# Attention in units of two heads on different rows of TensorE, and compression in four column groups

## The reference, cut to what matters

```python
# per layer; 4 MLA heads (96 for q and k), 4 differential heads of 2 maps (32), 8 NSA heads in 2 groups (64)
mla:   p = softmax(causal(q_h . k_h));                o_h = p @ v_h
diff:  p_m = softmax(causal(q_hm . k_hm)), m = 0, 1;  o_h = (p_0 - lam * p_1) @ v_h;  o_h = rms_norm(o_h) * (1 - lam_init)
nsa:   k_cmp, v_cmp = compress(k), compress(v)        # 31 blocks of 32 tokens, step 16
       o_cmp = softmax(q_h . k_cmp_g) @ v_cmp_g
       o_slc = softmax(causal(q_h . k_slc_g)) @ v_slc_g   # all 8 blocks of 64 tokens are selected at 512 tokens
       o_win = softmax(causal(q_h . k_win_g)) @ v_win_g
       o_h   = gate_0 * o_cmp + gate_1 * o_slc + gate_2 * o_win
compress: silu(blocks(31, 32*64) @ w1(2048, 256) + b1) @ w2(256, 64)    # for 2 groups, keys and values
out = concat(mla, diff, nsa) @ w_out
```

## Time and profile before

| | |
|---|---|
| median of 3 runs | 4109.87 us (4105.91 to 4119.1) |
| the profiled execution | 4141.39 us, span 4139.6 us |
| TensorE busy | 3912.5 us, 95% |
| VectorE, ScalarE, GpSimdE busy | 1468.9, 1291.3, 1271.3 us |
| mean granted TensorE clock | 0.93 |
| attention of layer 0, from its first score to its last value product | 603.3 to 925.9 us |
| attention of layer 1 | 1910.1 to 2222.8 us |

### The profile page before, as it was taken

How to read it: one execution, slowest core, us unless ns; L and a number is a source line. 1 busy time by engine, 2 the same in 40 slices (tenths; PEclk the granted TensorE clock), 3 DMA queues, 4 the chain that set the end, 5 groups by cost and what they waited for, 6 DMA issues and landing times. The chain is left out here.

```text
span 4139.6 us, 51715 instructions
## 1 busy us (share of the span) xinstructions
PE 3912.5 (95%) x18310; PEld 3064.2 (74%) x18310; DVE 1468.9 (35%) x2542; ACT 1291.3 (31%) x1995; POOL 1271.3 (31%) x524
## 2 busy tenths in 40 slices
PE   7998999999999999899999999699999898878998
PEld 6887666668887888656667888588888686557886
DVE  4224445444224322444445332611111602453112
ACT  4223233324223322313333322421212324334222
POOL 4444220004444444321001444222222242003443
PEclk9999996779999999997679999899999899989999
DMA  4333232102333333323111333222221232002331
GB/s 131 97 97 90 77 103 82 52 26 87 96 97 97 92 96 92 91 78 102 62 62 46 97 96 91 67 64 63 61 61 56 61 87 76 26 21 79 97 97 62
DMA packets 568999, 322.45 MB, mean 78 GB/s; under 512 B 30234, under 2 KB 563328, under 8 KB 568448
## 3 DMA queue, kind: packets, MB, share of 16 engines
q1 hardware_dynamic: 568832, 320.29, 26.5%
HBM read 318.14 MB, written 2.10 MB: 77 GB/s over the span
## 5 line engine op out<-in xcount | busy, mean ns | idle before, releaser
L796 POOL TENSOR_TENSOR w_lo<-w_raw,w_hi 128x1024 fp32r<-128x1024 f32 x516 | 1267.5, 2457 | 2833.3 <-ACT w_hi L807 2833.3
L807 ACT ACTIVATE w_hi<-w_raw 128x1024 fp32r<-128x1024 f32 x516 | 546.8, 1060 | 1901.2 <-PE psum L2001 1817.5
L2001 PE MATMUL psum<-h_hi,w_hi 128*128 128x512 f32 x1328 | 542.9, 409 | 46.2 <-DVE h_ctx_lo L1362 22.1
L2001 PE MATMUL psum<-xg_hi,w_hi 128*128 128x512 f32 x1408 | 551.7, 392 | 11.9 <-DVE xg_lo L1315 10.2
L2001 PE MATMUL psum<-xg_lo,w_hi 128*128 128x512 f32 x1408 | 548.9, 390 | 0.0
L2001 PE MATMUL psum<-xg_hi,w_lo 128*128 128x512 f32 x1408 | 548.8, 390 | 0.0
L2001 PE MATMUL psum<-h_lo,w_hi 128*128 128x512 f32 x1328 | 528.6, 398 | 0.0
L2001 PE MATMUL psum<-h_hi,w_lo 128*128 128x512 f32 x1328 | 526.6, 397 | 0.0
L2001 PE MATMUL psum<-a_hi,w_hi 128*128 128x512 f32 x1232 | 433.3, 375 | 4.9 <-DVE a_lo L1430 4.2
L2001 PE MATMUL psum<-a_lo,w_hi 128*128 128x512 f32 x1232 | 434.1, 375 | 0.0
L2001 PE MATMUL psum<-a_hi,w_lo 128*128 128x512 f32 x1232 | 432.6, 374 | 0.0
(11 more groups left out here) (407 smaller groups left out, 4767.7 us busy)
## 6 DMA issues: line engine op xcount, KB each, us to landing
w_raw<-ffn_w SPq DMA_DIRECT2D x120, 512.0 KB, 3.8
w_raw<-ffn_w_gate SPq DMA_DIRECT2D x88, 512.0 KB, 3.8
w_raw<-ffn_w_up SPq DMA_DIRECT2D x88, 512.0 KB, 3.8
ada_raw<-ada_w SPq DMA_DIRECT2D x72, 512.0 KB, 4.5
w_raw<-ffn_w_down SPq DMA_DIRECT2D x64, 512.0 KB, 4.2
w_raw<-w_in SPq DMA_DIRECT2D x60, 512.0 KB, 3.8
w_raw<-ffn_w_down SPq DMA_DIRECT2D x32, 384.0 KB, 3.4
w_raw<-w_out SPq DMA_DIRECT2D x24, 512.0 KB, 4.0
```

The costliest lines, as they stand in the source:

```text
L796: nc.gpsimd.tensor_tensor(w_lo[:, i, :], w_raw[:, i, :], w_hi[:, i, :].bitcast(F32), ALU.subtract).then_inc(lo_ready, 1)
L807: nc.scalar.activation(w_hi[:, pos, :], w_raw[:, pos, :], ACT.Copy).then_inc(hi_ready, 1)
L2001: last = nc.tensor.matmul(dst, w[:, pos, k * P:(k + 1) * P], rhs[g][r](k0 + k), start=k == 0 and m == 0, stop=k == nk - 1 and m == 2)
```

## The change

Heads are grouped by four (`GROUPS`), and a step handles a unit of two of them, chosen so that they stand on different rows: the two maps of a differential head, or one NSA head of each group. MLA heads go two at a time as well. There are 14 units per token block and 56 per layer. The order within a block is now MLA, differential, selected, window, selected, window.

```diff
+GROUPS = ([("mla", 0, [(h, 0) for h in range(MLA_H)])]
+          + [("diff", h0, [(h0 + j, m) for j in range(2) for m in range(2)]) for h0 in (0, 2)]
+          + [(kind, c0, [(4 * g + c0 + j, 0) for j in range(2) for g in range(NSA_G)]) for c0 in (0, 2) for kind in ("slc", "win")])
+NG = len(GROUPS)
+UN = 2 * NG
+NU = UN * TT
-ADA_AT = {6 * i + 1: i for i in range(ADA_SLOTS // 2)}
+ADA_STEPS = [UN * i + at for i, steps in enumerate(((5, 12), (2, 6, 9, 13), (2, 5, 8, 10, 13), (1, 3, 5, 7, 9, 11, 13))) for at in steps]
-AT_TURN, AT_CMP, AT_DIFF = 3, 6, 14
+AT_CMP, AT_CMP_EXP, AT_TURN, AT_CMP_TURN, AT_CMP_O, AT_DIFF = 1, 3, 5, 6, 8, 10
+def copy_on_dve(u):
+    return u % 4 == 3
```

Banks: scores of units and of the compressed attention alternate between banks 0, 1 and 2, 3. Everything that is transposed (units, finished rows, compressed probabilities) and the compressed product share banks 4 and 5, one after the other; each waits until the one before it has been copied out. Bank 6 holds the outputs of four heads, bank 7 the ada products. On TensorE:

```diff
+                for t in range(NU + 3):
+                    i, step = divmod(t, UN)
+                    if t < NU:
+                        v = SCORE_AT["unit", t]
+                        if v >= 2:
+                            pe.wait_ge(*scores_read(layer, v - 2))
+                        n = (i + 1) * P
+                        banks = [psum[:, score_banks(("unit", t)) + m, :] for m in range(2)]
+                        for m, head in enumerate(unit_maps(t)):
+                            q, k, _ = key_values(*head)
+                            nc.tensor.matmul(banks[m][:, 0:n], q(slice(i * P, (i + 1) * P)), k(n), start=True, stop=False)
+                        for m in range(2):
+                            last = nc.tensor.matmul(banks[m][:, n - P:n], ident_b[:], causal_b[:], start=False, stop=True)
+                        last.then_inc(scores_done.sem, 1)
...
+                    u = t - 2
+                    if 0 <= u < NU:
+                        pe.wait_ge(*exp_ready(layer, u + 1))
+                        x = TURN_AT["unit", u]
+                        if x:
+                            pe.wait_ge(*turn_read_out(layer, x - 1))
+                        for m in range(2):
+                            for b in range(u // UN + 1):
+                                last = nc.tensor.transpose(psum[:, 4 + m, b * P:(b + 1) * P], probs[:, u % 2, m, b * P:(b + 1) * P], ident[:])
+                        last.then_inc(probs_turned.sem, 1)
+                    if t < NU:
+                        if step == AT_TURN and i > 0:
+                            turn_o(layer, i - 1)
+                        if step == AT_CMP_TURN:
+                            pe.wait_ge(*cmp_exp(layer, i + 1))
+                            pe.wait_ge(*turn_read_out(layer, TURN_AT["cmp", i] - 1))
...
+                    u = t - 3
+                    if u >= 0:
+                        w = u // 2
+                        pe.wait_ge(*probs_copied(layer, u))
+                        if u % 2 == 0 and w:
+                            pe.wait_ge(*o_read_out(layer, w - 1))
...
+                    if t in ADA_AT:
...
```

The compressed scores go into the scores' banks at step 1, the compressed transposes at step 6, their product at step 8, `turn_o` at step 5; the ada product stands at the end of its step, and its short matmuls at the end of the next. `mixer_output` also waits for the last ada read. VectorE takes the maxima of a unit in one instruction over two banks, and the factors and outputs by four heads:

```diff
+                    dve.wait_ge(*exp_ready(layer, 2 * w + 2))
+                    nc.vector.reciprocal(factor, exp_sum[:, cols]).then_inc(inv_ready.sem, 1)
...
+                        nc.vector.tensor_tensor(pairs, pairs, by, ALU.mult).then_inc(inv_ready.sem, 1)
...
+                    nc.vector.tensor_tensor(weighted[:], o, wide(factor), ALU.mult).then_inc(inv_ready.sem, 1)
...
+                        nc.vector.tensor_tensor(dst, weighted[:].rearrange("p (j g) d -> p j g d", g=NSA_G), dst, ALU.add).then_inc(o_ready.sem, 1)
...
+                        nc.vector.tensor_reduce(neg_max[:, 2 * t:2 * t + 2], psum[:, b:b + 2, 0:(i + 1) * P], AX_X, ALU.max,
```

ScalarE does the two exponentials of a unit one by one, and the copy of both transposed banks as one instruction for three units of four; VectorE copies the fourth:

```diff
+                        if not copy_on_dve(u):
+                            if u >= 2:
+                                act.wait_ge(*o_done(layer, u - 1))
+                            n = (u // UN + 1) * P
+                            nc.scalar.activation(probs_t[:, u % 2, :, 0:n], psum[:, 4:6, 0:n], ACT.Copy).then_inc(probs_t_act.sem, 1)
```

Compression: taps are padded from 31 to 32 blocks, each of the four matmuls of a step (pair even or odd, group 0 or 1) has its own 32 output partitions, and the even and odd sums are added in the product that turns them:

```diff
-                            last = nc.tensor.matmul(psum[0:NC, 4 + g, 0:CMP_HID], taps[:, g, pair, :], aux[:, n % AUX_RING, j * CMP_HID:(j + 1) * CMP_HID],
-                                                    start=pair == 0, stop=pair == PAIR_TAPS - 1)
+                            at = CMP_BLOCK * (2 * (pair % 2) + g)
+                            last = nc.tensor.matmul(psum[at:at + CMP_BLOCK, 4, 0:CMP_HID], taps[:, g, pair, :], aux[:, n % AUX_RING, j * CMP_HID:(j + 1) * CMP_HID],
+                                                    start=pair < 2, stop=pair >= PAIR_TAPS - 2)
...
-                        for g in range(2):
-                            last = nc.tensor.transpose(psum[:, 6, (half * 2 + g) * 32:(half * 2 + g) * 32 + NC], hid_rows[:, g, half * P:(half + 1) * P],
-                                                       ident[0:NC, 0:NC])
+                        last = nc.tensor.matmul(psum[:, 6, half * 2 * CMP_BLOCK:(half + 1) * 2 * CMP_BLOCK], hid_rows[:, half * P:(half + 1) * P], fold[:],
+                                                start=True, stop=True)
```

More of the change, by code:

```diff
@@ L91, with copies_until, inv_before @@
 COND_M = 32
-assert max(ADA_AT) + 3 < ATT and ADA_SLOTS % ADA_RING == 0 and ADA_K * COND_M == P
-AT_TURN, AT_CMP, AT_DIFF = 3, 6, 14
+assert len(ADA_AT) == ADA_SLOTS // 2 and max(ADA_AT) + 1 < NU + 3 and ADA_SLOTS % ADA_RING == 0 and ADA_K * COND_M == P
+AT_CMP, AT_CMP_EXP, AT_TURN, AT_CMP_TURN, AT_CMP_O, AT_DIFF = 1, 3, 5, 6, 8, 10
+SCORE_ORDER, TURN_ORDER = [], []
+for _t in range(NU + 2):
+    _i, _s = divmod(_t, UN)
+    if _t < NU:
+        SCORE_ORDER.append(("unit", _t))
+        if _s == AT_CMP:
+            SCORE_ORDER.append(("cmp", _i))
+    if _t >= 2:
+        TURN_ORDER.append(("unit", _t - 2))
+    if _t < NU:
+        for _at, _kind, _of in ((AT_TURN, "o", _i - 1), (AT_CMP_TURN, "cmp", _i), (AT_CMP_O, "cmp_o", _i)):
+            if _s == _at and _of >= 0:
+                TURN_ORDER.append((_kind, _of))
+TURN_ORDER.append(("o", TT - 1))
+SCORE_AT = {item: n for n, item in enumerate(SCORE_ORDER)}
+TURN_AT = {item: n for n, item in enumerate(TURN_ORDER)}
+def copy_on_dve(u):
+    return u % 4 == 3
+def copies_until(u):
+    return sum(copy_on_dve(n) == copy_on_dve(u) for n in range(u + 1))
+INV_STEPS = {"mla": 1, "diff": 3, "slc": 3, "win": 3}
+def inv_before(w):
+    return sum(INV_STEPS[GROUPS[n % NG][0]] for n in range(w))
 MIX_Y = KD
@@ L211, in build @@
         rotate = put("rotate", [P, 2, P])
+        fold = put("fold", [P, 2 * CMP_BLOCK])
         ident_b = put("ident_b", [P, P], BF16)
@@ L434, in build @@
         gate_step = signal("gate_step", 2)
[L435 to L445, removed]
+        scores_done = signal("scores_done", NU + TT)
+        max_ready = signal("max_ready", NU)
+        exp_ready = signal("exp_ready", NU)
+        probs_turned = signal("probs_turned", NU)
+        probs_t_act = signal("probs_t_act", sum(not copy_on_dve(u) for u in range(NU)))
+        probs_t_dve = signal("probs_t_dve", sum(copy_on_dve(u) for u in range(NU)))
+        o_done = signal("o_done", NU)
+        inv_ready = signal("inv_ready", inv_before(TT * NG))
+        o_ready = signal("o_ready", TT * NG)
+        ada_read = signal("ada_read", ADA_SLOTS)
+        ada_turned = signal("ada_turned", ADA_SLOTS // 2)
         cmp_step = signal("cmp_step", 7 * TT + 2)
@@ L1335, in _ @@
             nc.vector.tensor_copy(ident_b[:], ident[:])
+            nc.vector.tensor_tensor(fold[:], ident[:, 0:P // 2], ident[:, P // 2:P], ALU.add)
             nc.vector.tensor_copy(causal_b[:], causal[:])
@@ L2239, in turn_o @@
             def turn_o(layer, i):
[L2241 removed]
+                pe.wait_ge(*turn_read_out(layer, TURN_AT["o", i] - 1))
+                pe.wait_ge(*o_ready(layer, (i + 1) * NG))
                 pe.wait_ge(*diff_ready(layer, i + 1))
                 pe.wait_ge(*cmp_o_ready(layer, i + 1))
[L2244 removed]
+                for b, rows in enumerate((o_first[:, i % 2, :], o_nsa[i % 2][:])):
                     for c in range(4):
[L2246 removed]
+                        last = nc.tensor.transpose(psum[:, 4 + b, c * P:(c + 1) * P], rows[:, c * P:(c + 1) * P], ident[:])
                     last.then_inc(o_turned.sem, 1)
@@ L2278, in attention @@
-                        if step == AT_CMP + 4:
+                        if step == AT_CMP_TURN:
                             pe.wait_ge(*cmp_exp(layer, i + 1))
-                            for g in range(2):
-                                last = nc.tensor.transpose(psum[:, 7, g * P:(g + 1) * P],
+                            pe.wait_ge(*turn_read_out(layer, TURN_AT["cmp", i] - 1))
+                            for g in range(NSA_G):
+                                last = nc.tensor.transpose(psum[:, 4, g * P:(g + 1) * P],
```

318 lines of the change are left out of this document (166 added, 152 removed).

## The result

The changed kernel takes 3907.14 us, median of 4 runs (3896.72 to 3916.25), against 4114.49 for the kernel before (4 runs, 4105.91 to 4143.18). The ratio is 0.947, 95% interval 0.943 to 0.950. Forecast was 3894. The profiled executions differ by more than the medians: 3899.32 (span 3897.3) against 4141.39, 242 us where the medians give 207.

The account below looks back on a forecast made before the run. TensorE was taken to bound the kernel, slowed by a low granted clock in attention. Gains of 175 us in attention and 41 in compression, 216 in all, took the median from 4109.9 to 3894 us; range 3830 to 3985.

Parts of the forecast that it names:

- What bounds the stage: Attention stages: TensorE sets the time, busy 319.4 of 322.6 us and 308.6 of 312.7 us.
- Scores in pairs: Attention: 24 heads' scores per token block become 12 overlapping pairs, gaining 35 us per layer at 2.4 GHz, 66 at 1.2.
- The clock: Attention: more rows at work leave a quarter of the stage at 1.2 GHz, granted clock near 0.88.
- Added waits, 20 us per layer: Attention pipeline: uncovered copies, VectorE at small n, exponential waits, fill and drain add 0 to 40, taken as 20 us.
- the three places: Per token block, o-transposes, compressed transposes and compressed products wait for the copy just begun: 8 us less what n = 1 hides.
- Compression, 41 us: Projections: compression matmuls in four column groups, four in 0.50 instead of 1.78 us: 20.5 us per layer, 41 in all.
- The sum: Whole kernel: attention gain 175 us plus compression 41 makes 216 us; 3925 us profiled, 3894 us as the median.
- Evacuation takes over: Rival: every unit's copy is uncovered, not three per block, 45 us more per layer: 3984 us, chance 0.07.
- Old clock share: Rival: attention's clock stays as it was, falls beginning at differential heads; gain 98 us: 4012 us, chance 0.18.
- No overlap: Rival: the paired scores don't overlap and only compression gains: 4119 us, chance 0.03.
- Full clock throughout: Rival: attention runs at full clock, 209 us a layer, gain 258 us: 3852 us, chance 0.15.
- The chain without overlap: Slower rival: each attention unit's steps run one after the other, 424 us a layer: 4281 us, chance 0.03.

Follow-up runs that it names:

- the 128-row versions: Differential and NSA head scores read all 128 rows, for timing only: in the kernel before 3982.94 us (0.965), in the changed kernel 3916.74 us (0.947).
- The kernel with the old compression: Changed kernel with compression as before (four matmuls of a step one behind the other, two-bank copy, four transposes): 3942.12 us, ratio 0.954.
- the two better ones: Changed kernel with value products ahead of the three special turns, 3878.25 us; the same with ada products at every third unit, 3872.69 us.
- the doubled copies: Changed kernel with each ScalarE copy of the turned probabilities issued twice, the second after the first: 3952.99 us, ratio 0.956.
- the best version: Changed kernel with value products ahead of the special turns and ada products evenly at every third unit: 3872.69 us, ratio 0.935.
- units with serial scores: Changed kernel with each head's causal product right behind its own score, keeping a pair's scores apart: 4183.15 us, ratio 1.013; with even ada 4154.95 us.

## Why the prediction was right

**What bounds the stage.** As it said: TensorE, before and after.

**Scores in pairs, 35 us per layer at full clock.** Right, and by the rows at every size: 1.06, 0.84, 0.63 and 0.42 us for a pair, the times of one score, sum 2.95 (forecast 2.9). The Trainium skill, TensorE: Matmul & The Clock Gate, section "Packing small matmuls", gives four 32-row tiles 3.07x; two row groups of 512 columns here give 2.11 / 1.06 = 2.0x, so the prediction's estimate of 27 us, carried over from it to pairs, was too low.

**The clock.** Right in mechanism and the largest term. Forecast: 0.88 granted and a loss of 42 us for both layers by halving. Measured: 0.94 and 0.93 and 55 us cold, a loss of 25. The two forecast figures don't agree with each other: 0.88 over a stage of 230 us is 55 us at 1.2 GHz, and half of that without the share of the added waits is 25 us per layer, not 21. The step "1.2 GHz takes twice the time" was wrong by its own rows (1.88): it put the loss of before at 181 us where 0.46 x 366 gives 168, and so the work at full clock at 227 instead of 233. The gain from the clock came out near all the same, 139 forecast and 143 measured; two errors of opposite sign made it so, a loss of before put too high and a stage after that was warmer than forecast. That rows at work are what pulls it was an argument from which heads were cold; the 128-row versions show it, in both kernels. The rest of the forecast for serial work, had the pairs not overlapped (4119 us), was too kind: the clock would have gone lower, to 4183.

**Added waits, 20 us per layer.** The mechanism was right, the three places named and found (10.3 us with the copies named). The size was too large: TensorE's idle time grew by 11 us. The 7 us that VectorE was to cost at n = 1 don't show. TensorE meets a late maximum as a wait for the exponential behind it, and those waits are 2.7 us in the whole stage, 0.7 of them at n = 1, where all idle time is 3.5 us. At full clock attention so gained 26 to 32 us per layer instead of 18; this is the term of the sum that was mis-sized.

**Compression, 41 us.** Right: 1.00 us for eight matmuls, and 20.4 us earlier at layer 0's attention, twice 41. The rest of the span shrank by 35. The other 6 are for the most part a cost that was not foreseen: at the end of each attention stage the drain (the last units' products and outputs, with no scores beside them) is followed by 6.8 us at 1.2 GHz that reach into the output projection, the last window above, 3 us a layer. The kernel with the old compression has that cost too: from its layer 0 attention to its layer 1 attention it takes 987.5 us, 20 to 22 more than the changed kernel's two profiles (968.0 and 965.7), while the kernel before takes only 15.5 more than the first of them. Forecast for that: nothing. TensorE's timeline of the changed kernel there, with the idle time ahead of two rows in brackets:

```profile
791.60 3.68 PE L2425 MATMUL psum<-v_win,probs_t 128*128 128x64 f32 x32
796.44 0.66 PE L2352 MATMUL psum<-ident,o_first 128*128 128x128 f32 x4 [1.15 <-DVE o_nsa L1766]
...
799.42 0.79 PE L2106 MATMUL psum<-h_hi,w_hi 128*128 128x512 f32 x1 [1.90 <-DVE h_lo L1713]
```

**The sum.** Between the profiles: 143 (clock) + 64 (work and waits) + 35 (rest) = 242 us, against 216 forecast; the 26 more are nearly all in the waits and the halving. Between the medians it is 207, since the profiled execution of before stood 27 us above its median and that of the changed kernel 8 below. The prediction left the first of these out of the difference; single runs of the kernel before spread over 45 us beside the last group, those of the changed kernel and the two better ones over 20 to 41, so a difference between two profiles has an error of some tens of microseconds. That the median fell within 13 us of the forecast is therefore in part luck: the terms were off by +4 (clock), +28 (work and waits) and -6 (rest), and the 26 us that they missed together were more than made up by the distance of the two profiles from their medians.

**Rivals.** Evacuation takes over: refuted by the doubled copies. Old clock share: refuted by 0.94. No overlap: refuted by the rows of the pairs. Full clock throughout, 3852, is nearly what the best version does in attention. The chain without overlap did not come.

**Left open.** Why units with serial scores are colder (253 and 253 us) than the single steps of before (195 and 171) with the same instructions to do. In the changed kernel, the stretch 614.0 to 627.7 stands at 0.50 though TensorE is busy for 13.1 of 13.7 us; ahead of it it had idled 2.1 us of 14, and it begins in the MLA units, whose scores stand on 96 rows. What starts and what ends such a stretch was not isolated. How far 32 rows are worse than 64 was not isolated either.

## What to carry to other kernels

When TensorE is busy nearly all the time and the granted clock is below 1.00, look at how many rows of the array its instructions fill before looking at their number: filling them by pairs brought back more here than the work saved. Operands on all rows kept the clock up as well, but here they held other heads' values; whether rows filled with zeros would do it was not run. Pair what stands on different row groups and issue the two back to back, with nothing between them. Where one buffer is shared, put the work that does not need it ahead of the wait for it: a few microseconds of idle time can cost several times as much when the clock falls with them (7 to 9 us per layer became 22 to 30 with the doubled copies).

## What the runs showed of the hardware

- fp32 matmuls of two row groups into two banks overlap wholly, 128 to 512 columns (0.42 to 1.06 us for two). One bf16 product of 0.16 us between them is enough to lose it.
- A fp32 score on 32 or 64 rows takes longer than one on 96 or 128 rows at the same 2.4 GHz: 1.05 against 0.91 us at 512 columns, 0.42 against 0.28 at 128.
- At 1.2 GHz a head's step takes 1.88 times as long, not twice.
- The same program with only the rows of its scores changed is granted 0.98 instead of 0.70, though TensorE idles more in it (11.9 against 3.2 us). Heads on 64 rows let the clock fall by themselves: with only they left below 128 rows, 150 us of the two stages are at 1.2 GHz, against 34. 7 to 9 us of added waits per layer brought the cold time of both layers from 62 to 143 us.
